# A trunk layer with experts on one core: raw tokens turned before they are normed, and the first expert's first two weight units given back by halves

## What is computed

```
mod = silu(c) @ w_mod + b_mod                      # six vectors of 1024: shift1, scale1, gate1, shift2, ...
hn  = rmsnorm(x, norm_mix_w) * (1 + scale1) + shift1
proj = hn @ w_in                                   # pooling columns, r/k/v and low-rank columns, merge gates
x   = x + gate1 * (gated pooling branch + gated two-way RWKV-7 scan) @ w_o
hn2 = rmsnorm(x, norm_ffn_w) * (1 + scale2) + shift2
x   = x + gate2 * sum over 32 experts of combine[:, e] * (act(hn2 @ w_gu[e] + b) @ w_down[e] + b)
```

## Time and profile before

| | |
|---|---|
| three runs, median | 1224.13 us (1222.58 to 1224.42) |
| profiled execution, own time | 1221.81 us |
| its span in the trace | 1220.0 us |
| TensorE (PE) busy | 1177.7 us, 97% |
| VectorE, ScalarE, GpSimd busy | 382.9, 192.4, 41.6 us |
| read from HBM | 462.37 MB, 380 GB/s over the span |
| chain that ended last | PE 74%, DMA 22%, VectorE 3% |

### The profile page before, as it was taken

The page is one execution under the profiler, slowest core; times in us unless marked ns, Lnnn a source line. Parts: engine busy times, 40 slices in busy tenths (PEclk is TensorE's granted clock), DMA queues, the critical chain, the costliest instruction groups (busy, mean ns, idle before and its releaser), DMA issues.

```text
span 1220.0 us, 17466 instructions
## 1 busy us (share of the span) xinstructions
PE 1177.7 (97%) x7087; PEld 557.1 (46%) x7087; DVE 382.9 (31%) x860; ACT 192.4 (16%) x363; POOL 41.6 (3%) x89
## 2 busy tenths in 40 slices
PE   6999999999999999999999999899999999999996
PEld 5777888987333333333333333333333333333333
DVE  2587984253421111122212211311112222122112
ACT  2350214201211111111211111111111111111002
POOL 5000210100000000000000000000000000000000
PEclk9999999999999999999999999999999999999999
DMA  9999230699999999999999999999999999999996
GB/s 331 325 380 354 71 112 34 209 393 405 385 429 429 428 429 428 428 429 429 428 429 428 427 407 427 427 428 430 429 428 429 427 427 430 429 429 428 429 427 256
DMA packets 73354, 464.37 MB, mean 381 GB/s; under 512 B 8375, under 2 KB 35662, under 8 KB 48094
## 3 DMA queue, kind: packets, MB, share of 16 engines
q1 hardware_dynamic: 70160, 458.12, 91.6%
q0 software_dynamic: 1504, 4.75, 1.1%
q10 hardware_dynamic: 1646, 0.86, 0.2%
HBM read 462.37 MB, written 1.34 MB: 380 GB/s over the span
## 4 chain that ended last, share of the span: by engine, by line
PE 74%; DMA 22%; DVE 3%; issue 1%; ACT 1%; ACTq 0%; DVEq 0%; SPq 0%
PE bank L1461 28%; DMA ring<-in_expert_w_gu 21%; PE bank L1578 12%; PE sums L809 5%; PE sums L1590 3%; PE sums L733 2%; PE sums L1265 2%; PE sums L1338 2%; PE sums L821 2%; PE bank L1373 2%; PE bank L1410 2%; PE sums L745 1%; PE bank L1558 1%; PE sums L945 1%; PE bank L709 1%
## 5 line engine op out<-in xcount | busy, mean ns | idle before, releaser
L1461 PE MATMUL bank<-ring,gate 128*64 128x512 f32 x1992 | 442.6, 599 | 14.5 <-DMA ring<-in_expert_w_gu 14.5
L1461 PEld LDWEIGHTS bank<-ring,gate 128*64 128x64 f32 x1992 | 139.9, 138 | 312.3 <-issue 282.1
L1578 PE MATMUL bank<-ring,gate 128*64 128x512 f32 x960 | 212.6, 595 | 3.3 <-DVE gate L2454 1.3
L2444 DVE TENSOR_SCALAR gate<-bank 128x512 f32<-128x512 f32 x31 | 21.4, 692 | 368.9 <-PE bank L1461 368.9
L1578 PEld LDWEIGHTS bank<-ring,gate 128*64 128x64 f32 x960 | 68.4, 137 | 126.8 <-issue 126.4
L1936 ACT ACTIVATE corr<-gate 128x512 f32<-128x512 f32 x31 | 19.5, 629 | 636.0 <-DVE gate L2444 636.0
L2460 DVE TENSOR_TENSOR corr<-bank,spare 128x512 f32<-128x512 f32 x31 | 21.4, 691 | 221.7 <-PE bank L1578 221.7
L1590 PE MATMUL sums<-corr,kk 64*128 64x512 f32 x248 | 61.6, 615 | 0.0
L1373 PE MATMUL bank<-qr,vt 128*64 128x512 f32 x248 | 58.5, 592 | 0.0
L809 PE MATMUL sums<-hnT,ring 128*128 128x256 f32 x256 | 56.4, 380 | 0.0
L809 PEld LDWEIGHTS sums<-hnT,ring 128*128 128x128 f32 x256 | 48.2, 190 | 7.1 <-issue 0.4
(11 more groups left out here) (440 smaller groups left out, 1048.1 us busy)
## 6 DMA issues: line engine op xcount, KB each, us to landing
ring<-in_expert_w_gu SPq DMA_DIRECT2D x122, 2048.0 KB, 19.3
ring<-in_expert_w_down SPq DMA_DIRECT2D x61, 2048.0 KB, 19.4
ring<-in_w_mod SPq DMA_DIRECT2D x16, 1024.0 KB, 9.9
ring<-in_w_in SPq DMA_DIRECT2D x13, 1024.0 KB, 10.4
ring<-in_w_mod SPq DMA_DIRECT2D x16, 512.0 KB, 9.9
ring<-in_expert_w_gu SPq DMA_DIRECT2D x5, 1024.0 KB, 18.4
ring<-in_w_in SPq DMA_DIRECT2D x9, 512.0 KB, 9.4
ring<-in_w_o SPq DMA_DIRECT2D x3, 1024.0 KB, 8.5
```

The source lines that it names most:

```text
L1461: last = mm(b[h * SLOTS:(h + 1) * SLOTS, :], xg[:, 2 * (u % 2) + i, u // 2, :], w(u, i, j, h), start=False, stop=(u == GU_UNITS - 1 and i ...
L1578: last = mm(DN[h * SLOTS:(h + 1) * SLOTS, :], actT[:, i, u, :], w(GU_UNITS + u, i // 2, i % 2, h), start=(u == 0 and i == 0), stop=(u == D ...
```

## The change

It has three pieces.

1. `x` is turned by 16 transposes as soon as it has landed. The scale is made apart: `ones` times the two diagonals gives, in bank 2, a row of the scales on every partition. ScalarE copies it to `junk`, and VectorE multiplies banks 7, 4, 6 and 5 with it on their way to `hnT`. L1663 and L2035 then work in place in `hnT`. The matmul of L694, whose result nothing reads, is gone.
2. Both chunks of quarter 0's modulation stand together. For quarters 1 to 3 the places of the two chunks and of the turn are written as tables. The lora loads are issued behind B0 instead of ahead of it.
3. The first expert is written out in front of TensorE's loop. In its units 0 and 1 the first half (one slot) is read by G and L, then the second; each half has its own signal, and SP loads the same units of expert 1 in halves.

```
-        for c in range(8, AT["Q", 3] + 1):
+        for c in range(8, AT["B", 0] + 1):
             next_chunk(c)
...
-        with sp.Fori(1, FIRST) as it:
+        for u in range(NU):
+            if u in SPLIT:
+                for i in range(2):
+                    sp.wait_ge(S(("late_mm", "chunk_used")[i]), (AFTER["half0"], 1)[i] + u)
+                    sp.dma_start(ring[:, 2 * u + i, :], unit_src(1, u)[:, CW * i:CW * (i + 1)]).then_inc(S(f"slot{2 * u}_full"), 16)
+            else:
+                sp.wait_ge(S("chunk_used"), u + 1)
+                expert_unit(1, u)
+        with sp.Fori(2, FIRST) as it:
...
+        for s in range(NS):
+            pe.wait_ge(S(("x_in", "x1_in")[s]), 16)
+            for k in range(KT):
+                tr(turned(s, k), x[:, s, k * P:(k + 1) * P], ident[:])
...
-        mm(banks[2][:, :], ident[:], x[:, 0, 0:512], start=True, stop=True)
...
-            last = token_turn(s, (5, 7))
+            last = mm(banks[2][:, s * T:(s + 1) * T], ones[:], xn[:, s, 0:P], start=True, stop=True)
...
-                if c < 3 and n == 4:
-                    mod_quarter(c + 1, range(2))
-                if c < 3 and n == 5:
+                if c < 3 and n == (5, 4, 4)[c]:
+                    mod_quarter(c + 1, (0,))
+                if c < 3 and n == (6, 5, 4)[c]:
+                    mod_quarter(c + 1, (1,))
+                if c < 3 and n == (7, 6, 5)[c]:
                     quarter_turn(c + 1)
...
+        def first_expert():
...
+                if u in SPLIT:
+                    for i in range(2):
+                        up_part(u, G, 0, from_ring, (i,))
+                        up_part(u, L, 1, from_ring, (i,)).then_inc(S(("late_mm", "chunk_used")[i]), 1)
+                    continue
+                last = up_part(u, G, 0, from_ring)
+                if u < GU_UNITS - 1:
+                    up_part(u, L, 1, from_ring).then_inc(S("chunk_used"), 1)
+            last.then_inc(S("g_mm"), 1)
+            up_part(GU_UNITS - 1, L, 1, from_ring).then_inc(S("chunk_used"), 1)
+            behind_up(0, (), ())
...
+        act.wait_ge(S("front_mm"), AFTER["xnT"])
+        af(junk[:, 0, 0:TT], banks[2][:, 0:TT], ACT.Copy).then_inc(S("csig_ready"), 1)
...
-        v.tensor_copy(hnT[:].rearrange("p (k j) t -> p k j t", j=2)[:, 2:4, 1, :], banks[7][:, :].rearrange("p (k t) -> p k t", k=2)).then_inc(S("xn_ready"), 1)
+        dve.wait_ge(S("csig_ready"), 2)
+        def scaled(b):
+            j, g = (b - 4) // 2, (b - 4) % 2
+            return v.tensor_tensor(hnT[:].rearrange("p (k j) t -> p k j t", j=2)[:, 2 * g:2 * g + 2, j, :],
+                                   banks[b][:, :].rearrange("p (k t) -> p k t", k=2), bc(junk[:, 0, 0:TT], 2), MUL)
+        scaled(7).then_inc(S("xn_ready"), 1)
+        for b in (4, 6, 5):
+            step(scaled(b))
```

More of the change, by code:

```diff
@@ L46 @@
 IN_HALVES = (GU_UNITS - 1, NU - 1)
+SPLIT = (0, 1)
 ONCE = {9: (2, 3), 14: (1,), 22: (4, 5)}
@@ L372, in trunk_kernel @@
         ("prmT", "xnT", "prbT", "gate0", "gate1", "s0", "norm", "inorm", "vt0", "vt1", "rksum", "rk", "pooled", "mixed"),
-        ("grow", "mean", "var", "istd", "shift", "shiftb", "logits", "sums", "rank", "count", "pos", "list")) for i, n in enumerate(names)}
+        ("grow", "mean", "var", "istd", "shift", "shiftb", "logits", "sums", "rank", "count", "half0", "half1", "pos", "list")) for i, n in enumerate(names)}
     DONE = {n: i + 1 for i, n in enumerate(("shift", "rws", "sqsum", "r2", "sel", "top", "extra", "comb", "e16", "combT", "items"))}
@@ L413, in _ @@
         sp.dma_start(gw2, A["gate_w2"][0]).then_inc(S("lora_in"), 16)
-        for c in range(AT["Q", 3] + 1, AT["B", 1] + 1):
+        for c in range(AT["B", 0] + 1, AT["B", 1] + 1):
             next_chunk(c)
@@ L690, in _ @@
         pe.wait_ge(S("consts_ready"), IDENT)
+        for s in range(NS):
+            pe.wait_ge(S(("x_in", "x1_in")[s]), 16)
+            for k in range(KT):
+                tr(turned(s, k), x[:, s, k * P:(k + 1) * P], ident[:])
         pe.wait_ge(S("rows_a_in"), 96)
         tr(banks[3][:, 0:96], rows_a[:], ident[0:96, 0:96]).then_inc(S("front_mm"), 1)
-        pe.wait_ge(S("x_in"), 16)
-        mm(banks[2][:, :], ident[:], x[:, 0, 0:512], start=True, stop=True)
-        def token_turn(s, some):
-            for k in some:
-                last = mm(turned(s, k), x[:, s, k * P:(k + 1) * P], xn[:, s, 0:P], start=True, stop=True)
-            return last
         def mod_quarter(c, halves):
@@ L757, in _ @@
             pe.wait_ge(S("xn_ready"), s + 1)
-            last = token_turn(s, (5, 7))
+            last = mm(banks[2][:, s * T:(s + 1) * T], ones[:], xn[:, s, 0:P], start=True, stop=True)
         last.then_inc(S("front_mm"), 1)
-        for s in range(NS):
-            token_turn(s, (0, 1))
         pe.wait_ge(S("cpad_ready"), 1)
         pe.wait_ge(S("xn_ready"), 3)
-        mod_quarter(0, (0,))
-        for s in range(NS):
-            token_turn(s, (2, 3))
-        mod_quarter(0, (1,))
-        token_turn(0, (4, 6))
+        mod_quarter(0, range(2))
         quarter_turn(0)
-        token_turn(1, (4, 6))
         for c in range(4):
@@ L1516, in last_down @@
                         last.then_inc(S(("scattered_ctx", "scattered_lat")[s]), 1)
+        def first_expert():
+            pe.wait_ge(S("xg_ready"), 1)
+            for u in range(GU_UNITS):
+                pe.wait_ge(S(f"slot{2 * u}_full"), 16 * (FRONT_USES[2 * u] + 1))
+                if u == 1:
+                    pe.wait_ge(S("xg_rest"), 1)
+                if u in SPLIT:
[9 more added lines that the diff above has]
+            behind_up(0, (), ())
         def expert(it, skipped, outside=(), half=None, late=False, end=False):
@@ L1593, in _ @@
         pe.wait_ge(S("slot1_full"), 16 * (FRONT_USES[1] + 1))
-        with pe.Fori(0, FIRST) as it:
+        first_expert()
+        with pe.Fori(1, FIRST) as it:
             expert(it, ())
@@ L1662, in _ @@
             for s in range(NS):
-                last = af(hnT[:, k, s * T:(s + 1) * T], turned(s, k), ACT.Identity,
+                last = af(hnT[:, k, s * T:(s + 1) * T], hnT[:, k, s * T:(s + 1) * T], ACT.Identity,
                           bias=moda[:, 0, k, s:s + 1], scale=moda[:, 1, k, s:s + 1])
@@ L2033, in modulated @@
             for s in range(NS):
-                src = turned(s, k) if c < 2 else hnT[:, k, s * T:(s + 1) * T]
-                last = v.tensor_scalar(hnT[:, k, s * T:(s + 1) * T], src, moda[:, 1, k, s:s + 1], moda[:, 0, k, s:s + 1], MUL, ADD)
+                h = hnT[:, k, s * T:(s + 1) * T]
+                last = v.tensor_scalar(h, h, moda[:, 1, k, s:s + 1], moda[:, 0, k, s:s + 1], MUL, ADD)
             last.then_inc(S("hnd_ready"), 1)
+        last_of("xn_ready", 3)
         modulated(0)
```

5 lines of the change are left out of this document (3 added, 2 removed).

## The result

| | before | after |
|---|---|---|
| median of 22 runs each | 1222.88 us (1221.11 to 1224.71) | 1224.49 us (1223.09 to 1228.83) |
| ratio, 95% interval | | 1.0017 (1.0011 to 1.0022) |
| profiled execution, span | 1220.0 us | 1223.4 us |
| first part of quarter 0 | 19.16 us | 15.56 us |
| first expert | 311.88 us | 314.11 us |

The account below looks back on a forecast made before the run. The prediction took a DMA stream, full from the first expert on, to set the end. Gains of 1.2 us at the front and 1.4 us at the hole, 2.6 us, took 1224.13 to 1221.5 us; range 1219.7 to 1224.1.

Parts of the forecast that it names:

- The start of the parts: Front of quarter 0: with transposes and scaling on VectorE, the first part begins at 16.2 us, not 19.16, 2.9 us earlier.
- The clock: Start of TensorE's work: lower level up to 14 us, then parts at the higher level, 0.216 us a pass.
- The rival that had this fall: Clock falls while TensorE idles between second chunk and first part; costs 1.8 us, giving 1223.3 us; chance 0.20.
- The reason against it: Against a clock fall ahead of quarter 0's parts: before, TensorE stood 0.94 us and parts at 19.16 us ran higher.
- The tables: Ahead of quarters 1 and 2: TensorE stands 1.35 and 0.5 us, taking 1.2 and 0.5 us from the front's gain.
- The hole: DMA stream at the first expert, 312 to 320 us: 2.65 us lost, of which halves win back 1.4 us.
- What was costed at nothing: Lora loads, moved behind B0, and VectorE's other work: wanted only after 50 us, so priced at zero.
- The slower rival: Front: clock rises too late after transposes and gaps; up to 8.8 us more, 1225.9 to 1230 us; chance 0.09.

Follow-up runs that it names:

- front_only: The changed kernel with the first expert in the loop again, without the written-out expert and its halves; 1226.52 us, ratio 1.0027 to the kernel before.
- old_tables: The changed kernel with both chunks of the next quarter's modulation behind part 4 again and the turn behind part 5; 1222.21 us, ratio 0.9996 to before.
- tables_only: The kernel before with only the three tables, for the places of both chunks and the turn in quarters 1 to 3; 1225.72 us, ratio 1.0025.
- light_new: The changed kernel plus two unused matmuls: 256 columns behind the `ones` products, 512 behind quarter 0's turn; 1222.80 us, ratio 1.0000 to before.
- light_old: The changed kernel with the modulation's old places and two unused matmuls (256 columns behind the `ones` products, 512 behind quarter 0's turn); 1220.23 us, ratio 0.9980 to before.
- turn_late: The kernel before with only the turn of quarters 1 to 3 at later places, both chunks staying behind part 4; 1224.61 us, ratio 1.0017.
- late_unit: The kernel before with expert 1's unit 0 issued one unit of reading later, together with unit 1; 1226.36 us, ratio 1.0029.
- light_ones: The changed kernel with the modulation's old places and one unused matmul of 256 columns behind the `ones` products; 1220.56 us, ratio 0.9985 to before.
- busy: The changed kernel with eight unused matmuls in the four places where TensorE stands ahead of the first part; 1225.46 us, ratio 1.0015 to before.

## Why the prediction was wrong

- **The start of the parts** was right in its steps, and early in the trace: 15.56 us against 16.2. The transposes, the `ones` products and the copy came as forecast; a product of L2040 took 0.62 us, not 0.69; the second chunk began at 12.23 us behind its landing and ran at the higher level, so that `moda` was begun at 14.14, not 14.9. That is a gain of 3.6 us instead of 2.9 over the execution that the forecast was worked out from, and of 2.8 to 3.2 over the other executions of the same front: its size was right. Nor is 15.56 us the rule: `front_only` began at 16.59, `old_tables` at 16.26.
- **The clock** is the step that failed. The sum took the higher level for granted from about 14 us on. It was there, before 10.26 us, and it fell again at 14.4 us. The rival that had this fall named the place where it lies in this trace (the idle time between the second chunk and the first part) and was given 0.20; in `front_only` the fall came before it and in `old_tables` behind it. Its price was one fall of 1.8 us; it was 8.2 - 5.4 = 2.8 us in the changed kernel, since the level stayed down over more of the parts than in the row it was priced from the earlier trace rows, and 6.24 - 4.55 = 1.7 us in `old_tables`. The reason against it, that at 19.16 us TensorE had stood for 0.94 us without a fall, compared a shorter stand, and that one alone. In `tables_only` a single stand of 1.40 us at the same place was followed by no fall either; in the changed kernel three others come ahead of the one of 1.53 us. That these count together is argued from this, not shown: filling the last alone was enough (`light_turn`), but in `front_only` the level fell with stands of 1.25 and 0.62 us alone behind it. Taking the fall away gives 2.1 us (`light_new` against the changed kernel); `light_old` is 2.0 us better than `old_tables`, with the doubt stated above. The kernel before had a matmul whose result nothing reads at its start (L694), which the change took out; whether it would have kept the level up in the new front wasn't tried.
- **The tables** were the second failure, of size: 1.7 us forecast, 2.9 in quarters 0 and 1, and 3.1 by the ratio of `tables_only`. The stands themselves were right (1.46 and 0.66 us against 1.35 and 0.5). The late turn came to 2.2 us: 0.15 us were taken off for a loss that the old order doesn't have (its passes go on without a gap), the stands are 0.13 us longer in `turn_late`, and 0.2 us come besides them. Left out altogether was that two groups of matmuls cut into four lose 0.7 to 1 us.
- **The hole** was right in mechanism, and the stream does set the end, as `late_unit` shows. Of the 1.4 us the stretch behind the first expert shows 0.4 to 1.1 in two kernels and 0.7 from mean to mean, the way to the last expert 0.5, and the times 0.9. Not all of the 2.65 us was a lack of work: in the kernel before, the DMA engines were 83 to 102% busy from 312 to 315 us and moved 307 to 350 GB/s there. By the working of the prediction that is 0.7 us, ahead of the first half's issue. The step "a half keeps the stream busy for 2.45 us, longer than the 1.74 us to the second half" held only in part: the stream dipped to 175 GB/s at 320.25 us, some 4 us behind the first half's issue.
- **What was costed at nothing**, the lora loads, showed a worth of 0.3 us, and only in a front that is earlier than the changed kernel's.
- The slower rival, a clock that rises too late, didn't come: it rose early. The Trainium skill, page "TensorE: Matmul & The Clock Gate", section "Part 4: PE-mode transpose", says that transposes don't engage the higher level. This case's trace disagrees: the four passes of L763 at 8.37 us took 0.64 us, against 1.11 us for the same passes in `light_old` (L768, at 8.57 us), and ahead of them TensorE had done nothing but 16 transposes and the turn of the parameter rows. That it isn't the time alone shows before the change: TensorE began at 8.28 us, and its 16 passes from 10.23 us on still took 3.62 us, against 8 in 1.16 us later.

With their measured sizes the terms are -3.6 + 2.8 + 2.9 = +2.1 us at the first expert (2.2 in the trace), and -0.4 for the halves in this execution: +1.7 us, where the times say 1.6 to 2.1. How well that fits is partly luck, since the start of single executions moves by as much as 1.5 us. The forecast was a gain of 2.6 us, worked out from a median of 1224.13 us for the kernel before, which is 1222.88 over 22 runs; gain against loss it was off by 4.2 to 4.7 us, of which the fall of the clock is 2.1 to 2.8, the tables 1.2 and the hole 0.3 to 1.0.

`light_turn`, the change with the old places of the modulation and one matmul of 512 columns behind quarter 0's turn, is the fastest of all by its median, and faster than both kernels of the change: 1219.88 us, 0.9978 (0.9969 to 0.9988), 2.7 us under the kernel before. What holds it next are transfers: it waits 1.00 us for A3 in quarter 0, 0.5 us for `w_mod` at 101 us and 0.6 us for `w_rwkv_out`.

## What to carry to other kernels

A step that makes TensorE's inputs ready earlier may leave it with less to do, and the stretch that follows can then run at the lower level: list all the stands ahead of it, and ask what a matmul without use would save; put it only where TensorE would wait anyway. A turn or reduction whose result another engine must apply wants parts behind it that cover the whole way back, and a long group of matmuls is worth more in one piece. Before a forecast is worked out from one execution, look at how its first steps vary between executions. When a stream of transfers sets the end, the hole is best measured by the bytes that moved in a fixed stretch from the same event, since its start and its rate change together, and over more than one execution.

## What was not expected of the hardware

- The level rose while TensorE had done transposes alone: 16 of them took 3.34 us here, against 3.65 us in executions in which it rose later (`light_old`), and what follows ran at twice the pace (0.64 against 1.11 us).
- The fall came at different times in executions of the new front: at 12.3 us in `front_only`, at 14.4 in the changed kernel, and, with the old places, at 15.0 in `light_ones` and at 16.9 in `old_tables`.
- The added matmul of 512 columns, 1.02 us in a stand of 1.8 us, held the granted clock at 1.00 where it had been 0.50.
- A stand of 1.46 us was followed by a fall in `busy` (20 passes in 6.24 us) and by none in `light_new` and the changed kernel (4.55 us).
